# Reordered splits, taps and norms, and one wait less, in a float32 attention and Hyena kernel

## The reference, cut to what matters

```python
merged = (jax.nn.sigmoid(g_diff) * (o_diff @ w_proj_diff[layer])
          + jax.nn.sigmoid(g_mla) * (o_mla @ w_proj_mla[layer]))
x = x + merged @ w_out[layer]
return rms_norm(x, norm_final)
```

```python
h = (h @ _f32(f_wout)).reshape(L, 2, D_MODEL)
h = h * jnp.exp(-t * jnp.abs(deltas))[:, None, :]
kern = jnp.concatenate([h[:, 0], jnp.zeros((1, D_MODEL), jnp.float32), h[:0:-1, 1]], axis=0)
return kern / jnp.sum(jnp.abs(kern), axis=0, keepdims=True)
...
y = (y + z * _f32(bias)).astype(u.dtype)
```

## Time and profile before

| | |
|---|---|
| median of 3 runs | 1120.66 us (1119.62 to 1123.31) |
| profiled execution | 1120.66 us, of it 1118.9 us span |
| granted TensorE clock, mean | 0.987 |
| TensorE busy | 1065.9 us, 95% of the span |
| VectorE, ScalarE, GpSimd busy | 60%, 37%, 48% |

### The profile page before, as it was taken

How to read it: one execution, slowest core, us unless ns; L and a number is a source line. 1 busy time by engine, 2 the same in 40 slices (tenths; PEclk the granted TensorE clock), 3 DMA queues, 4 the chain that set the end, 5 groups by cost and what they waited for, 6 DMA issues and landing times.

```text
span 1118.9 us, 13388 instructions
## 1 busy us (share of the span) xinstructions
PE 1065.9 (95%) x4970; PEld 866.8 (77%) x4970; DVE 671.3 (60%) x1011; ACT 414.3 (37%) x643; POOL 540.5 (48%) x399
## 2 busy tenths in 40 slices
PE   6999989999899999969999989989999999999996
PEld 5889876767677878757788877867888888888885
DVE  6652758776468863966568893358666666630203
ACT  5223646454455244453443323243232332321211
POOL 1059799999300045343444334543655555464441
PEclk9999999999999999979999999989999999999999
DMA  6246355242344841230222223222223223222421
GB/s 246 76 152 238 104 198 173 95 156 89 141 169 163 340 167 53 104 113 1 113 76 76 76 76 145 82 94 76 76 76 150 76 75 109 116 76 76 151 76 75
DMA packets 17991, 131.98 MB, mean 118 GB/s; under 512 B 2305, under 2 KB 2705, under 8 KB 11410
## 3 DMA queue, kind: packets, MB, share of 16 engines
q1 hardware_dynamic: 8784, 93.74, 22.3%
q0 software_dynamic: 6560, 27.27, 7.4%
q10 hardware_dynamic: 2594, 10.25, 2.3%
HBM read 124.96 MB, written 6.29 MB: 117 GB/s over the span
## 4 chain that ended last, share of the span: by engine, by line
PE 84%; DVE 8%; DMA 3%; ACT 2%; issue 2%; POOL 0%; SPq 0%; ACTq 0%; POOLq 0%; DVEq 0%
PE bank L491 71%; PE bank L482 6%; PE bank L497 2%; DMA ring<-weights_in 2%; PE bank L712 2%; PE bank L710 1%; PE bank L709 1%; DVE arena L2013 1%; DVE arena L2016 1%; DMA x_sb<-x_in 1%; ACT arena L1096 0%; ACT ring_parts L1096 0%; PE bank L714 0%; ACT arena L1234 0%; ACT arena L1119 0%
## 5 line engine op out<-in xcount | busy, mean ns | idle before, releaser
L1606 POOL TENSOR_TENSOR ring_parts<-ring,ring_parts 128x1024 fp32r<-128x1024 f32 x102 | 247.9, 2434 | 306.7 <-ACT ring_parts L1096 305.2
L1096 ACT ACTIVATE ring_parts<-ring 128x1024 fp32r<-128x1024 f32 (+2 forms) x163 | 168.6, 1042 | 478.8 <-PE bank L491 299.1
L491 PE MATMUL bank<-hT_parts,ring_parts 128*128 128x512 f32 x1344 | 340.4, 394 | 0.5 <-ACT hT_parts L1393 0.5
L491 PEld LDWEIGHTS bank<-hT_parts,ring_parts 128*128 128x128 f32 x1344 | 250.4, 189 | 54.4 <-issue 2.4
L491 PE MATMUL bank<-ring_parts,arena_parts 128*128 128x512 f32 (+1 forms) x736 | 172.4, 386 | 1.5 <-DVE arena L2231 0.8
L491 PE MATMUL bank<-ring_parts,hT_parts 128*128 128x512 f32 (+1 forms) x672 | 171.3, 382 | 2.7 <-ACT ring_parts L1096 1.8
L491 PEld LDWEIGHTS bank<-ring_parts,arena_parts 128*128 128x128 f32 x736 | 136.5, 188 | 29.7 <-DVE arena L2231 1.3
L491 PE MATMUL bank<-arena_parts,ring_parts 128*128 128x512 f32 x592 | 148.6, 392 | 2.6 <-DVE arena L1811 2.3
L491 PEld LDWEIGHTS bank<-ring_parts,hT_parts 128*128 128x128 f32 x672 | 123.6, 190 | 26.4 <-issue 3.0
L2331 DVE SCALAR_TENSOR_TENSOR arena<-bank,small,arena 128x441 f32<-128x441 f32 (+2 forms) x176 | 122.3, 695 | 23.8 <-DVE arena L2326 0.3
L491 PEld LDWEIGHTS bank<-arena_parts,ring_parts 128*128 128x128 f32 x592 | 111.7, 189 | 28.1 <-DVE arena L1811 2.5
(11 more groups left out here) (224 smaller groups left out, 1101.7 us busy)
## 6 DMA issues: line engine op xcount, KB each, us to landing
ring<-weights_in SPq DMA_DIRECT2D x39, 2048.0 KB, 8.0
arena<-mod_w_in POOLq DMA_DIRECT2D x32, 512.0 KB, 3.9
arena<-mod_w_in POOLq DMA_DIRECT2D x8, 1024.0 KB, 5.0
x_sb<-x_in SPq DMA_DIRECT2D x4, 512.0 KB, 5.6
ring<-weights_in SPq DMA_DIRECT2D x4, 512.0 KB, 8.5
mod_spill<-mod_part POOLq DMA_DIRECT2D x16, 128.0 KB, 2.1
x_sb<-x_in ACTq DMA_DIRECT2D x4, 512.0 KB, 11.3
arena<-mod_spill ACTq DMA_DIRECT2D x1, 2048.0 KB, 10.1
```

The source lines that it names most:

```text
L491: ins = nc.tensor.matmul(out, l, r, start=start and n == 0, stop=stop and n == len(passes) - 1)
L1096: return nc.scalar.activation(out, in_, ACT.Copy)
L1606: return nc.gpsimd.tensor_tensor(part(low), low, part(high), ALU.subtract)
```

## The change

It reorders work, moves one small product to another bank and another place, lets the merge keep its product in SBUF, and removes one wait. By engine:

- VectorE: `MOD_AFTER` gets 10 for 17, and a modulation chunk comes ahead of a net layer at the same piece. The merge's first operation writes to `sgm` in place of the bank; three splits of `w_out` pieces lie behind steps 2, 4 and 6. `add_abs(6)` goes ahead of `scale_n2(2)`. `add_abs(7)` goes ahead of `norm_x2(3)`. `bias_tap(1)` goes to the head of the Hyena part.
- TensorE: `abs_norm(1)` moves from behind the eight turns to between `modulation(2)` and `modulation(3)`, into bank 4.
- ScalarE: three splits go ahead of three DMA issues; `wout_split(0)` goes into the merge; `abs_out(7)` goes ahead of two splits.
- GpSimd: `sum_wout(0)`, with its wait for `fout`, goes ahead of the `sgd_low` subtractions; all four `hyz` splits go behind the last roots, without the wait for `modc_ready`.

```diff
@@ -65,7 +65,7 @@
 MOD_POOL_COLS = 128
 MOD_POOL = 4 * D // MOD_POOL_COLS
 MOD_DVE_COLS = 256
-MOD_AFTER = (9, 11, 13, 15, 16, 17, 18, 19)
+MOD_AFTER = (9, 10, 11, 13, 15, 16, 18, 19)
 ROOTS_AFTER = (7, 18, 21, 23, 25)
 UQ_W, UKV_W = 768, 1024
 MOD_DVE = 2 * D // MOD_DVE_COLS
@@ -388,7 +388,7 @@
 
             return {"n1": 0, "n2": KD, "n3": 2 * KD}[tag] + k + 1
 
-        NORM_BANK = (2, 1)
+        NORM_BANK = (2, 4)
         N2_BANKS = (1, 2)
         N3_BANKS = (4, 5, 6, 7)
 
@@ -908,6 +908,7 @@
             filter_tile(7)
             wo_tile(7)
             modulation(2)
+            abs_norm(1)
             modulation(3)
 
             def transform(b, tables, cos_in, sin_in):
@@ -961,7 +962,6 @@
 
             def second_spectrum():
                 pe.wait_ge(sem("n2_full"), KD)
-                abs_norm(1)
                 taps_spectrum(1)
 
             def norms_by_channel(i):
@@ -1289,14 +1289,13 @@
             wait("gate_done", 12)
             for m in range(TT):
                 act.dma_start(x_sb[:, m, :], x_d[m * P:(m + 1) * P, :]).then_inc(sem(f"x_in{m}"), 16)
-            split_high(FIRST_PD + 4)
+            for p in range(FIRST_PD + 4, FIRST_PD + 8):
+                split_high(p)
             wait("mod_dve_done", MOD_DVE)
             act.dma_start(mod_back, mod_spill_d).then_inc(sem("mod_back_in"), 16)
             act.dma_start(mod_part[:], tables_d[:, 2048:2304]).then_inc(sem("tables_in"), 16)
             wait("h3_ready", 1)
             act.dma_start(deltas, deltas_d.partition_broadcast(P).rearrange("p a d -> p (a d)")).then_inc(sem("deltas_in"), 16)
-            for p in range(FIRST_PD + 5, FIRST_PD + 8):
-                split_high(p)
 
             def wout_split(n):
                 wait("wout_sum", 2 * n + 2)
@@ -1307,6 +1306,8 @@
                 copy(part(hT[:, d, :]), sgd[:, d, :]).then_inc(sem("sgd_high"), 1)
                 if d % 2:
                     split_high(FIRST_WO + d // 2)
+                if d == 4:
+                    wout_split(0)
 
             wait("deltas_in", 16)
 
@@ -1343,7 +1344,6 @@
 
             decay_out(0)
             decay_out(1)
-            wout_split(0)
             wout_split(1)
             modg_copy(0)
             wait("modc_done", 1)
@@ -1365,9 +1365,9 @@
                 if m < 2:
                     decay_out(6 + m)
                 square_x2(m)
+            abs_out(7)
             split_high(FIRST_HYZ)
             split_high(FIRST_HYZ + 1)
-            abs_out(7)
             square_x1(TT - 1)
             split_high(FIRST_HYZ + 2)
             modg_copy(2)
@@ -1638,26 +1638,22 @@
                 wait("wout_high", n + 1)
                 subtract(wout[n], wout_high[n]).then_inc(sem("wout_low"), 1)
 
+            wait("fout_in", 16)
+            sum_wout(0)
             for d in range(KD):
                 wait("sgd_high", d + 1)
                 subtract(sgd[:, d, :], hT[:, d, :]).then_inc(sem("sgd_low"), 1)
-            wait("fout_in", 16)
-            sum_wout(0)
             low_wout(0)
             sum_wout(1)
             low_wout(1)
             for p in range(FIRST_WO + PIECES, FIRST_HYZ):
                 split_low(p)
             for m in range(TT):
-                if m == TT - 1:
-                    split_low(FIRST_HYZ)
-                    split_low(FIRST_HYZ + 1)
                 wait("squares_done", squares_at("x1", m))
                 rsqrt(RS + m, SS + m, 1, D, "x_rs")
                 wait("squares_done", squares_at("x2", m))
                 rsqrt(RS2 + m, SS2 + m, 1, D, "x2_rs")
-            wait("modc_ready", 1)
-            for p in range(FIRST_HYZ + 2, FIRST_HYZ + PIECES):
+            for p in range(FIRST_HYZ, FIRST_HYZ + PIECES):
                 split_low(p)
             for i in range(16):
                 if i and i % 2 == 0:
@@ -1967,12 +1963,12 @@
             wait("cond_ready", 1)
             for p in range(FIRST_GATE + 6, FIRST_PD + 4):
                 split_low(p)
+                if p - FIRST_GATE in MOD_AFTER:
+                    mod_chunk(MOD_AFTER.index(p - FIRST_GATE))
                 if p == FIRST_GATE + 8:
                     split_output(UNITS - 1)
                 if p - FIRST_GATE - 8 in NET_AFTER:
                     net_layer(NET_AFTER.index(p - FIRST_GATE - 8))
-                if p - FIRST_GATE in MOD_AFTER:
-                    mod_chunk(MOD_AFTER.index(p - FIRST_GATE))
 
 
             wait("net_out", 4)
@@ -1987,11 +1983,10 @@
             for d in range(KD):
                 wait("merge_done", KD + d + 1)
                 wait("merge_out", KD + d)
-                link(V.tensor_tensor(bank[d], sgm[:, d, :], bank[d], ALU.mult))
-                V.tensor_tensor(sgd[:, d, :], sgd[:, d, :], bank[d], ALU.add).then_inc(sem("merge_out"), 1)
-                if d in (3, 5):
-                    split_low(FIRST_WO + (d - 3) // 2)
-            split_low(FIRST_WO + 2)
+                link(V.tensor_tensor(sgm[:, d, :], sgm[:, d, :], bank[d], ALU.mult))
+                V.tensor_tensor(sgd[:, d, :], sgd[:, d, :], sgm[:, d, :], ALU.add).then_inc(sem("merge_out"), 1)
+                if d in (2, 4, 6):
+                    split_low(FIRST_WO + d // 2 - 1)
             split_low(FIRST_WO + 3)
 
 
@@ -2093,11 +2088,11 @@
             scale_taps(7)
             scale_n2(1)
             norm_x2(2)
+            add_abs(6)
             scale_n2(2)
             add_wo(7)
-            add_abs(6)
+            add_abs(7)
             norm_x2(3)
-            add_abs(7)
             scale_n2(3)
             modulation()
 
@@ -2247,11 +2242,11 @@
                 V.scalar_tensor_tensor(out=x, in0=y, scalar=st(RNORM + i), in1=x, op0=ALU.mult,
                                        op1=ALU.mult).then_inc(sem("y_out"), 1)
 
+            bias_tap(1)
             taps_groups(0)
             wait("modc_ready", 1)
             wait("x_spilled", 16 * TT)
             input_full("n2", 0, N2_BANKS, x_low)
-            bias_tap(1)
             input_low("n2", x_low)
             taps_groups(1)
             for i in range(4):
```

## The result

The changed kernel took 1130.01 us (median of 5 runs, 1128.07 to 1132.52), the kernel before, on the same chip, 1122.03 (1119.62 to 1123.31). The ratio of the two is 1.0090, 95% interval 1.0068 to 1.011: about 10 us slower (7.6 to 12.3). The forecast was +6.0 us, so it has the sign and falls short in size. (The forecast was made against the profiled execution of the kernel before, 1120.66, which lies 1.4 us under this median.)

A forecast was written before the change was run, and what follows sets the result against it. TensorE was taken as the bound, busy 1065.9 of 1118.9 us, so only its idle stretches could give time back. The terms 1.1 + 3.0 + 1.9 = +6.0 on 1120.66 gave 1126.7, stated as 1126.5 us, range 1117 to 1130.

The forecast's parts named there:

- Part 1: Gate loop, `MOD_AFTER` and order: the moved modulation chunk delays TensorE's second filter layer, +1.1 us (bounds 0 to 1.3).
- Part 2: Merge and first `w_out` tile, 392 to 422 us: late loads and GpSimd subtractions delay VectorE, +3.0 us (0 to 4.5).
- the late chunk: First `w_out` chunk, beside ScalarE's moved loads: lands about 2.5 us later, at 403.
- the pile-up: Merge: GpSimd waits for `fout` until 406, then its eight `sgd_low` subtractions run without gaps until about 423.
- Part 3: 476 to 512 us: a 5.2 us gain, but splits block four VectorE operations; net +1.9 us (−5.2 to +3.4).
- The gain stays: Rival: splits don't hold up `modc` and `bias_tap(1)`, merge finds its gaps; −4.1, 1116.5 us; chance 0.18 (under 1118).
- Gain and merge cost cancel: Rival: Part 3 gives its 5.2, Part 2 costs its 3.0; −1.1, 1119.5 us; chance 0.14 (1118 to 1122).
- Half blocked: Rival: Part 3 −0.5 to +1, Part 2 one or two; +3, 1123.7 us; chance 0.16 (1122 to 1124).
- worse: Rival: full merge waits, low clock in Part 3; 1.3 + 4.5 + 3.4, 1129.9 us; within the 0.52 for 1124.0 and up.
- the full waits of the merge: Upper bound of Part 2: every VectorE operation in the merge draws the full wait for a GpSimd subtraction, +4.5 us.

The follow-up runs named there:

- p3_modc: Kernel before with only Part 3's edits, but the wait for `modc_ready` put in front of all four GpSimd `hyz` splits: 0.9948 (0.9925 to 0.9972).
- undo_modc: The changed kernel with GpSimd's wait for `modc_ready` put back in front of the four `hyz` splits: 1.0000 (0.9981 to 1.0018) to the kernel before.
- best: Kernel before with Part 3's reorder, `modc_ready` wait kept, `modg_copy(2)` and `(3)` ahead of ScalarE's splits, two bias operations behind `input_full`: 0.9939, median 1115.68 us.
- p3_guard: Kernel before with only Part 3's edits, but GpSimd's four splits held back behind both `bias_tap(1)` operations: 0.9948 (0.9927 to 0.9969).
- p2_no_dma: Kernel before with only Part 2's edits, but ScalarE's loads left where they were: 1.0019 (0.9990 to 1.0047).
- p3_only: Kernel before with only Part 3's edits, the wait for `modc_ready` removed: 1.0011 (0.9992 to 1.0029).

## Why the prediction was right or wrong

**Part 1, +1.1: right.** TensorE waits 1.14 us before the second filter layer; alone the part gave +1.0, within the noise.

**Part 2, +3.0: the wait right, its price short, its cause half right.** TensorE's wait is 4.89 us, +3.04. The chain of it in the changed kernel, ScalarE, VectorE, then GpSimd:

```profile
404.84 1.06 ACT L1096 ACTIVATE ring_parts<-ring 128x1024 fp32r<-128x1024 f32 x1 [4.16 <-DMA ring<-weights_in]
...
420.29 1.04 ACT L1096 ACTIVATE ring_parts<-ring 128x1024 fp32r<-128x1024 f32 x1
```

```profile
405.93 1.23 DVE L1722 TENSOR_TENSOR ring_parts<-ring,ring_parts 128x1024 fp32r<-128x1024 f32 x1 [3.19 <-ACT ring_parts L1096]
...
410.13 2.29 DVE L1722 TENSOR_TENSOR ring_parts<-ring,ring_parts 128x1024 fp32r<-128x1024 f32 x1
...
415.77 2.28 DVE L1722 TENSOR_TENSOR ring_parts<-ring,ring_parts 128x1024 fp32r<-128x1024 f32 x1
```

```profile
408.30 3.04 POOL L1634 TENSOR_TENSOR arena<-arena 128x512 f32<-128x512 f32 x2 [43.62 <-DMA arena<-weights_in]
411.30 14.24 POOL L1606 TENSOR_TENSOR arena_parts<-arena,hT_parts 128x512 fp32r<-128x512 f32 x8
```

The chunk was in at 404.84, where I had said 403, and `fout` at 408.30, where I had said 406. The step that I didn't see: `split_low(FIRST_WO)` now stands before step 3 in VectorE's queue, so VectorE itself stands for the late chunk, 3.19 us. I had followed only the third split to its new place, and of the two late transfers only `fout`, to GpSimd. Behind that the subtractions do run back to back as forecast, even at 1.78 us each (14.24 for eight), and two of the splits take 2.28 us instead of 1.2, the additions 0.88 to 1.07 instead of 0.69. But the table says that without the pile-up the price is the same, and that the pile-up without the late chunk gives 1.76. So it was partly luck that the wait came out at +3.0.

The term that was mis-sized is what follows the wait. The clock fell at 420.2, during the wait. The ten matmuls behind it take 4.61 us at half the clock, for 2.51 in the earlier trace rows, and until 427.0 the stretch loses 2.9 us more, so part 2 is +5.9 in the trace and +5.3 alone. In part 2 I had no half clock at all, and in part 3 only as an upper bound, though the earlier trace rows show one behind the 8.7 us of before. It goes with the length of the wait: of the sixteen traces of this case, all six with 3.59 us or more before these matmuls have them at half the clock, in part or all (3.67 to 4.61 us for the ten), but only three of the ten with 1.85 to 2.91 us (3.43 to 3.95).

**Part 3, +1.9: right in mechanism, near in size.** The gain is there: the squares of x1 begin at 487.36, 5.5 us earlier than the earlier trace rows shifted by the 6.2 of delay, TensorE's wait for `abs_norm(1)` is 4.11 where I had said 4, and `mod_g` is no longer waited for. The four splits then block VectorE:

```profile
493.29 2.83 DVE L2061 TENSOR_SCALAR arena<-x_sb,stat 128x1024 f32<-128x1024 f32 x1 [2.50 <-POOL stat L1538]
...
496.26 2.17 DVE L1999 SCALAR_TENSOR_TENSOR modc<-modc,small 128x8 f32<-128x8 f32 x2
...
499.06 2.13 DVE L2021 TENSOR_TENSOR arena<-arena,row 1x512 f32<-1x512 f32 x1
501.22 2.73 DVE L2024 TENSOR_TENSOR arena<-arena 1x512 f32<-1x512 f32 x1
...
507.79 1.52 DVE L2104 TENSOR_SCALAR x_sb<-bank,modc 128x512 f32<-128x512 f32 x2
```

```profile
493.23 10.18 POOL L1606 TENSOR_TENSOR ring_parts<-ring,ring_parts 128x1024 fp32r<-128x1024 f32 x4
```

I had `scale_n2(3)` go first; the splits began 0.06 us ahead of it, so it was blocked too, and the two `modc` operations shared one wait. That is four waits, as forecast, on partly other operations. `input_full` begins 9.36 us later than in the earlier trace rows, 3.2 without the 6.2 of delay; I had said 3.8. The new wait at the third turn is 3.82 us, not 8: TensorE ran at half the clock from 485.0 to 498.7, so the first spectrum began late and took 5.62 us for 4.55 before, and that hid the rest. The turns behind it again run at half the clock (1.6 us), which I had as a bound. Together +2.7.

**The rivals.** "The gain stays" was the kernel with the wait left in: −5.8 for `p3_modc`, for which I had −5.2 as the end of the range of part 3. "Gain and merge cost cancel" is what `undo_modc` gives: 1.0000. "Half blocked" had part 3 at −0.5 to +1: alone it measured +1.2 and can't be told from that, in the changed kernel it cost 2.7. The changed kernel landed at the bound of the rival "worse", 1129.9, partly through other terms than that one's: the half clock at the third turn was in it, the full waits of the merge (+4.5) didn't come, and the half clock behind the merge and at two places far behind came in their stead.

**What failed is one step:** the sum took each new wait at its own length, and the matmuls behind it at nothing. In the two traces 1.1 + 3.0 + 1.1 (part 3 without its slow turns) = 5.2 us are what the sum had at 6.0. Another 2.9 and 1.6 are matmuls at half the clock right behind the two new waits: part 2 costs 5.9 us and not 3.0, part 3 2.7 and not 1.9. And 3.4 more fall near 556 and 659, in code that wasn't touched. They don't look like the chance of one trace: the mean granted clock is 0.979 to 0.982 in the 14 runs of the changed kernel, 0.981 on average, and 0.984 to 0.987 in the ten of `undo_modc`, 0.985 on average. By my estimate one spell of 3.4 us in 1131 us lowers it by 0.0015, so the runs differ by two or three spells, and the one at the third turn is one of them. Why the change brings the others isn't settled: the same wait of 2.47 us before L482 is followed by half the clock in eleven of the sixteen traces, `best` among them, and not in the other five (before, `p3_guard`, `p3_modc`, `p2_no_dma`, `undo_modc`).

## What to carry to other kernels

Before a wait on one engine is taken out, look at which operations of the other engine it kept apart: here four long GpSimd splits set free 1.3 us early (485.59 in `p3_only`, 486.85 in `p3_modc`) cost two small VectorE operations and a scaling 4 us on the path, and one wait decides 7 to 10 us. When a new wait of several us appears on TensorE, price the matmuls behind it at both clock levels from rows, not the wait alone. And when work is moved in a queue behind a transfer, follow every instruction behind it in that queue, not only the one that reads the data.

## What the hardware showed that I had not expected

- **The scatter of one kernel goes with the clock.** The 35 runs of the kernel before, averaged by their mean granted clock: 0.988 gives 1120.2 us (2 runs), 0.987 1121.6 (6), 0.985 1122.7 (12), 0.984 1123.8 (7), 0.982 1127.8 (8). A spell of 3.4 us at half the clock costs about 1.7 us (5.41 for 3.72 near 556), so by my estimate the whole range is that of four or five such spells. The changed kernel's 14 runs lie at 0.982 (1130.1 on average) to 0.979 (1135.4).
- **Operations of 0.2 us wait for whole splits.** Two `modc` operations of 128x8 took 2.17 us for both beside a split, 0.24 without one; a row of 1x512 took 2.13 and 2.73, 0.68 without (`p3_guard`). This is the exclusion that the Trainium skill, "SBUF — State Buffer", section "Who interferes with whom", states for instructions with two SBUF inputs; the trace agrees. `scale_n2(3)`, with a single tensor as its input, took 2.83 us for 0.76 beside a split too; the split had begun 0.06 us earlier.
- **Additions with both operands in SBUF took 0.80 to 1.79 us where they met GpSimd's subtractions (1.3 us and more), 0.69 with one in PSUM.** They lost at most the length of one subtraction, as bounded, and most of them less.
